# Half of the modulation units of the first attention placed between the levels of the gated recurrence

## The reference

```python
for l in range(DEPTH):
    mod_lat = (jax.nn.silu(c) @ w_mod[l] + b_mod[l])[:, None, :]
    mod_ctx = (jax.nn.silu(c_ctx) @ w_mod[l] + b_mod[l])[None, None, :]
    sh1, sc1, g1, sh2, sc2, g2 = jnp.split(mod_lat, 6, axis=-1)
    ...
    h_lat = rms_norm(x, norm_pre_mix[l]) * (1.0 + sc1) + sh1
    if l % 2 == 0:
        y_lat, y_ctx = even_mixer(...)   # grouped attention and gated recurrence, then w_out
    ...
    x = x + g1 * rms_norm(y_lat, norm_post_mix[l])
    h_lat = rms_norm(x, norm_pre_ffn[l]) * (1.0 + sc2) + sh2
```

## Time and profile before

| | |
|---|---|
| time, median of 3 runs | 3439.45 us (3438.46 to 3442.85) |
| profiled execution | 3442.54 us |
| its span | 3440.5 us |
| TensorE busy | 3270.0 us, 95% of the span |
| VectorE busy | 897.4 us |
| ScalarE busy | 691.1 us |
| GpSimd busy | 495.7 us |
| first attention, in the trace | 268.7 to 340.0 us |
| near levels, in the trace | 340.0 to 386.1 us |

### The profile page before, as it was taken

One profiled execution on the slowest core, in us unless ns is written; L12 is line 12 of the kernel. 1 busy time (PEld: TensorE's weight loads), 2 busy tenths in 40 slices (PEclk: granted clock), 3 DMA queues, 4 the chain that ended last, 5 costly groups with the idle time before them and its releaser, 6 DMA issues.

```text
span 3440.5 us, 81881 instructions
## 1 busy us (share of the span) xinstructions
PE 3270.0 (95%) x35194; PEld 2864.3 (83%) x35195; DVE 897.4 (26%) x1990; ACT 691.1 (20%) x1505; POOL 495.7 (14%) x441
## 2 busy tenths in 40 slices
PE   7999789999899999999999999989999999999998
PEld 5886678888786788787799887778899999988888
DVE  2324745553313321214233123130000110011001
ACT  2324122221204321212211011201111211101011
POOL 1210125555121010100057010000000000000000
PEclk9999689999899999999999999989999999999999
DMA  6546012222233244343344442238999999944477
GB/s 274 198 165 233 3 49 83 88 85 88 72 104 123 88 157 137 125 141 110 110 160 156 150 147 98 97 124 338 381 380 396 388 394 378 402 151 149 143 271 290
DMA packets 94204, 638.90 MB, mean 186 GB/s; under 512 B 10720, under 2 KB 11760, under 8 KB 36480
## 3 DMA queue, kind: packets, MB, share of 16 engines
q1 hardware_dynamic: 91472, 628.62, 49.2%
q0 software_dynamic: 2608, 8.49, 0.8%
HBM read 636.02 MB, written 1.05 MB: 185 GB/s over the span
## 4 chain that ended last, share of the span: by engine, by line
PE 89%; DMA 4%; DVE 3%; ACT 2%; issue 2%; POOL 0%; SPq 0%; ACTq 0%; DVEq 0%
PE bank L1109 18%; PE bank L663 18%; PE bank L618 12%; PE bank L781 12%; PE bank L802 5%; PE bank L634 5%; PE bank L719 4%; PE bank L1069 2%; DMA ring<-in_moe_down 2%; PE bank L566 2%; PE bank L592 1%; PE bank L1124 1%; PE bank L838 1%; DMA ring<-in_moe_up 1%; PE bank L820 1%
## 5 line engine op out<-in xcount | busy, mean ns | idle before, releaser
L781 PE MATMUL bank<-PROJ,ring 128*64 128x80 f32 (+1 forms) x7424 | 485.0, 257 | 11.6 <-DMA ring<-in_moe_down 7.7
L1109 PE MATMUL bank<-MIX,ring 128*64 128x80 f32 x12544 | 473.7, 235 | 21.1 <-issue 10.9
L1109 PEld LDWEIGHTS bank<-MIX,ring 128*64 128x64 f32 x12544 | 448.6, 138 | 47.0 <-issue 39.7
L781 PEld LDWEIGHTS bank<-PROJ,ring 128*64 128x64 f32 (+1 forms) x7424 | 441.8, 145 | 53.5 <-DMA ring<-in_moe_down 12.5
L618 PE MATMUL bank<-H,ring 128*128 128x256 f32 x1856 | 407.5, 382 | 4.1 <-ACT H L1297 4.1
L618 PEld LDWEIGHTS bank<-H,ring 128*128 128x128 f32 x1856 | 354.4, 192 | 56.7 <-issue 4.7
L1109 PE MATMUL bank<-H,ring 128*128 128x256 f32 x896 | 193.7, 379 | 0.0
L663 PE MATMUL bank<-H,ring 128*64 128x128 f32 (+1 forms) x1296 | 185.2, 331 | 5.4 <-ACT H L1297 4.7
L1109 PEld LDWEIGHTS bank<-H,ring 128*128 128x128 f32 x896 | 170.2, 190 | 23.4 <-issue 0.3
L663 PE MATMUL bank<-MIX,ring 128*64 128x128 f32 (+1 forms) x1272 | 181.1, 321 | 0.8 <-DVE MIX L1884 0.8
L802 PE MATMUL bank<-H,ring 128*128 128x256 f32 x768 | 178.0, 390 | 3.9 <-ACT PROJ L1396 3.7
(11 more groups left out here) (383 smaller groups left out, 3717.4 us busy)
## 6 DMA issues: line engine op xcount, KB each, us to landing
ring<-in_moe_up SPq DMA_DIRECT2D x224, 1024.0 KB, 7.2
ring<-in_moe_down SPq DMA_DIRECT2D x128, 896.0 KB, 6.3
ring<-in_up SPq DMA_DIRECT2D x44, 1024.0 KB, 4.8
ring<-in_mod_b SPq DMA_DIRECT2D x40, 1024.0 KB, 6.5
ring<-in_tproj SPq DMA_DIRECT2D x32, 1024.0 KB, 4.8
ring<-in_proj SPq DMA_DIRECT2D x26, 1024.0 KB, 4.8
ring<-in_gates SPq DMA_DIRECT2D x24, 1024.0 KB, 4.8
ring<-in_swup SPq DMA_DIRECT2D x22, 1024.0 KB, 4.8
```

The lines of the kernel that those rows point to most:

```text
L781: mm = pe.matmul(B[bank][lo:lo + m, 0:width], w[:, k, lo:lo + m], src(s * half + k), start=s == 0 and k == 0, stop=s == 1 and k == half - 1)
L1109: mm = pe.matmul(B[(t0 + 2 * j + t) % 4][lo:lo + m, 0:n], w[:, k, t * P + lo:t * P + lo + m], src[:, k, 0:n], start=k == 0, stop=k == KT - 1)
```

## The change

Nine units, 39 to 47, leave the attention. `MOD_H` puts three behind near level 1, two each behind levels 2, 3 and 4. The attention keeps units 30 to 38, one in each of the iterations 1, 3, 5, 7, 8, 10, 12, 14 and 15. The turn of unit 47 moves from the end of the attention to behind level 5. ACT copies the nine rows ahead of its first instruction of the recurrence. DVE reads the columns of units 8 to 37 after the attention and those of units 38 to 47 behind the take of level 5. TensorE writes to bank 5 in the near stretch only after DVE's first reading (`mod_ready` at 2), and gives bank 5 to head 3 of level 6 only after the second (`mod_ready` at 3). The users in layer 1 wait for 3 in place of 2. The order of the weights in the ring is the same.

```diff
+MOD_H = (0, 3, 2, 2, 2, 0)
...
         def mods_at(i):
             m = MOD_A + MOD_P
-            n = 48 - m
+            n = 48 - m - sum(MOD_H)
             return range(m + n * i // 16, m + n * (i + 1) // 16) if i < 16 else ()
+
+        def mods_near(i):
+            m = 48 - sum(MOD_H)
+            return range(m + sum(MOD_H[:i]), m + sum(MOD_H[:i + 1]))
...
-                    if l == 0 and i == n:
-                        mod_turn(47)
...
                 for h in range(B_HEADS):
                     pe.wait_ge(S("hg_x"), (i - 2) * B_HEADS + h + 1)
+                    if i == 6 and h == 3:
+                        pe.wait_ge(S("mod_ready"), 3)
...
             for i in range(6):
                 hgrn_near(i)
+                for m in mods_near(i):
+                    pe.wait_ge(S("mod_ready"), 2)
+                    mod_step(m)
+            mod_turn(47)
...
             def hgrn():
+                for i in range(6):
+                    for m in mods_near(i):
+                        mod_row(m)
                 act.activation(qw[:, :], eps, ACT.Sqrt)
...
-            act.wait_ge(S("mod_ready"), 2)
+            act.wait_ge(S("mod_ready"), 3)
...
-                dve.wait_ge(S("mod_ready"), 1 if i1 == 1 else 2)
+                dve.wait_ge(S("mod_ready"), 1 if i1 == 1 else 2 + l)
...
                     if i < 6:
                         take(i)
+                    if i == 5:
+                        mod_vectors(47 - sum(MOD_H), 48)
...
-            mod_vectors(MOD_A, 48)
+            mod_vectors(MOD_A, 47 - sum(MOD_H))
```

## The result

| | before | after |
|---|---|---|
| time, median of 5 runs | 3439.43 us (3437.68 to 3442.85) | 3456.22 us (3451.45 to 3459.42) |
| profiled execution, its span | 3442.54, 3440.5 us | 3457.13, 3455.3 us |

The kernel is slower: the ratio is 1.0044 with a 95% interval of 1.0031 to 1.0057. The forecast was 3451, with a range of 3436 to 3460.

A forecast was written before the change was run, and what follows sets the result against it. The prediction took instruction supply, one page of 256 instructions per 3.7 us, to leave TensorE barely ahead of DVE in the near levels. 21.6 us more there less 9.9 in the attention gave 11.7 slower: 3451 us, range 3436 to 3460.

The forecast's parts named there:

- The near levels, 21.6 us forecast: Near levels: nine moved steps, after their cover of supply stops, start the level after level 5 21.6 us later.
- Waits for ACT: Near levels, within a group: the turn waits for ACT's copy of the unit just done, 0.58 us together.
- Four groups: Near levels: a group of two costs 6.2 us, the group of three 9.6; all four 28.2 us.
- The end of level 5, 64.8 us forecast: Near levels: TensorE ends level 5 64.8 us after their start, where it was 42.4 before.
- the walk: Near levels, page by page: each 128-record page takes 3.7 us, or its content where that is longer.
- The terms listed behind the walk: After level 5: DVE's products 1.2 us, decays 0.39, take 0.73, new reading about 0.25; next level at 67.7.
- Clock: Near levels: steps and level matmuls together stay at 1.2 GHz, 1.93 us a unit; full-clock rival 3438 us, chance 0.15.
- The weight stream, priced at zero: Near levels: the 9 MB of weights loaded there were taken to slow instruction packets by zero.
- the rival: Near levels: the weight stream slows five instruction pages, 6 us more, 3457 us; chance 0.12.
- The attention, 9.9 us forecast: Attention: removing seven steps, two doubled steps and the turn of unit 47 saves 9.9 us.
- its own bounds of 8 to 15.3: Attention saving: 15.3 us with all nine steps at full price, waits and turn; 8 if ACT and DVE order slips.
- The step of iteration 0: Attention, iteration 0: removing its step saves nothing, since the 3.45 us chain through ACT's exponentials sets the length.

The follow-up runs named there:

- the spread steps: The kernel after the change with its nine near-level steps one at a time between heads instead of in groups behind whole levels: 3449.68 us, ratio 1.0025 to before.

## Why the prediction was right

- *The near levels, 21.6 us forecast, 21.8 measured.* The mechanism held: pages pace the levels, and groups at the lower clock come on top. Groups at 1.93 us a unit: right, each of the nine. Waits for ACT 0.58: 0.60. Four groups 28.2 us: 27.8. The second reading of columns is on the path, 0.1 us in place of 0.25.
- *The end of level 5, 64.8 us forecast, 65.0 measured.* That this came so close is in part luck, since two errors cancel. The first pages came faster than in the kernel before, and the first group started 11.9 us after the start of the near levels, 1.4 earlier than the walk had it. Against that, the page that holds the group behind level 3 took 9.8 us (374.07 to 383.84) where the walk had 7.5, its content: a stop of 2.16 us stood at its end. The run with a step in iteration 0 has the same page at 9.8 us. The instruction queue of the earlier trace rows moved no packet from 373 to 381 us, though the DMA engines were idle for the first 4 us of that page (busy time by stretch, columns as in the earlier trace rows):

```profile
374.00:378.00 4.00, 3.33 (x30) 1.97 (x31) 3.12 (x4) 0.38 (x1) 0.00 (x0) 0.50 0.01 2
378.00:381.00 3.00, 3.00 (x62) 2.05 (x66) 0.00 (x0) 0.27 (x1) 0.00 (x0) 0.50 0.90 306
```

  So a long page is not always its content, as the walk took it. Whether the load that began at 378 held the packet up, or TensorE asked for it late, no run tells. The terms listed behind the walk also add up to 67.4 and not to the 67.7 on record; 67.9 was measured.
- *Clock.* That steps and levels together stay at the lower level held for groups. The argument (neither alone brings the clock up, so both don't) was too strong: interleaved, they did in part. Its row was also read too widely: the stretch with 11.57 us busy of 12 holds the last of the eight units, and ahead of them TensorE had waited for weights, for 3.86 us once.
- *The weight stream, priced at zero.* Wrong as a statement on the chip: in the kernel before, the same 9 MB cost 7.7 us. As a term of this sum it was small at most, for which the prediction had no row: the pages clear of a group came 2.9 to 4.0 us after the one before, the longest of them from 370.06 to 374.07 with the DMA engines 47% busy, where 3.7 were booked. The stop at 383.84 may hold some of it. The price of 6 us for the rival was of the right size for a stream alone. That the measured 3456 lies by that rival's 3457 is chance: its 6 us in the near levels did not come, the attention's 4.1 did.
- *The attention, 9.9 us forecast, 5.8 measured.* This is the term that was mis-sized, by 4.1, and it lies outside its own bounds of 8 to 15.3. The step of iteration 0 was booked as "saves nothing". That step costs when it is taken away: without it TensorE stood idle for 2.3 us, the clock fell, and iterations 1 and 2 took 6.72 and 3.71 us, for 3.62 and 3.0. Five profiles here have that stop, and in them iteration 1 takes 5.2 to 6.7 us; with the step in iteration 0 it takes 3.62 in all that have one. No rival had the clock fall in the attention. The other iterations came near to what was worked out: 9 and 13 at 3.48 (3.45 forecast), 6 at 2.99 and 11 at 2.78 (2.7 and 2.4), and 4 saved 0.3, where nothing was forecast. With the step in iteration 0 in place of 15 the saving is 10.9.
- *The sum.* 11.7 forecast, 16.0 by the trace at the state updates, 16.8 by the medians. The direction and the larger term were right by their mechanism; the time is within the range, 5 us above the forecast, for the clock in the attention.

The Trainium skill ("Runtime: NRT & Kernel Launch", section on instruction fetch mechanics) calls page crossings mostly hidden. The traces disagree: in the kernel before they paced the near levels at 3.7 us a page, and with a weight stream beside them at 4.3. The prediction's walk, with one page held ahead, fits the first burst after the change too: 225 records, where 221 were worked out.

What stays open: how the 7.7 us of the spread steps part into stops and clock; by what way a weight load delays a page, and why one page stopped for 2.16 us behind a group; and why the last 2 to 5 us at the experts' counts don't reach the time with two units moved. The spread of the experts' stage is large enough to hide them; that it does was not shown.

## What to carry to other kernels

A busy share of 60% is not 40% of free time. Before work is moved into such a stretch, ask what the idle pieces wait for: here it was instructions. One step to a page came cheaper than groups, 57.3 us in place of 65.0, but both are far above the 42.4 without steps, since a step at the lower clock (2.8 us) is longer than the stops (up to 2.2 us). Only a step where TensorE was ahead of VectorE, behind level 5, was free. And look at what the moved work did where it was: a step that was hidden in a wait kept TensorE's clock up, and its removal cost more than it weighed.

## What the runs showed of the hardware

- Instructions for TensorE came in pages of 128 pairs of weight load and matmul. A page began 3.5 to 4.0 us after the one before without a weight stream, 4.34 in the mean with one at 68% of the DMA time, and single ones of 5.2 to 6 under a stream. After the change, with groups of steps, short pages came down to 2.9 us, and one that held a group took 9.8 with a stop of 2.16 us at its end.
- In five profiles TensorE stood for 2.3 us in iteration 0, and all had half clock at the latest 1.6 us behind it, for 3.4 to 10 us; in the seven profiles with a step there, and a stop of 0.78 us, iteration 1 ran at the full clock.
- Modulation units in groups between small matmuls all ran at 1.93 us; one at a time, three of nine ran at 1.07 and one at 1.57 in one kernel, two of nine at 1.07 in another. With dense matmuls beside them all nine ran at 1.07.
- One matmul of a unit took 1.06 us at the lower clock, and all eight of them 1.93.
- The granted clock reads 1.00 from 22 to 34 us, where the units take 1.93 us, the duration of the lower level. The durations decide.
